# A decoder block on one core: the weight panel's split between the second and third eviction, and the experts' semaphores raised before the attention stage

## What is computed

```python
h = rms_norm(x, g_mix)
z = h @ w_in                      # 1024 x 8208, split into ten column groups
q, k, v, r, a_lr, c_b, c_c, c_x, g_a, g_b = split_columns(z)
o = gla_chunked(q, k, v, log_sigmoid(a_lr @ w_alpha_up + b_alpha) / 16)
y_a = (rms_norm(o, g_gla) * silu(r)) @ w_branch_a
y_b = (c_b * causal_dwconv(c_c * c_x, w_conv)) @ w_branch_b     # 3 taps
x = x + (sigmoid(g_a) * y_a + sigmoid(g_b) * y_b) @ w_out
h = rms_norm(x, g_ffn)
x = x + top-4-of-32 mixture of experts(h)    # clamped SwiGLU, chosen pairs alone
out = rms_norm(x, g_final)
```

## Time and profile before

| | us |
|---|---|
| median of 3 runs | 2753.02 (2749.55 to 2753.60) |
| the profiled execution | 2757.46, its span 2755.8 |
| PE busy | 2550.3 (93%) |
| DVE busy | 1502.2 (55%) |
| ACT busy | 1205.3 (44%) |
| convolution, first panel's last eviction to last panel's | 624.71 to 952.73 |
| join | 955.8 to 1260.3 |
| route, up to its closing barrier | 1260.4 to 1333.7 |
| experts | 1337.3 on |

### The profile page before, as it was taken

One profiled execution on the slowest core, in us unless ns is written; L12 is line 12 of the kernel. 1 busy time (PEld: TensorE's weight loads), 2 busy tenths in 40 slices (PEclk: granted clock), 3 DMA queues, 4 the chain that ended last, 5 costly groups with the idle time before them and its releaser, 6 DMA issues. The chain is left out here.

```text
span 2755.8 us, 41814 instructions
## 1 busy us (share of the span) xinstructions
PE 2550.3 (93%) x14459; PEld 2041.2 (74%) x14460; DVE 1502.2 (55%) x1470; ACT 1205.3 (44%) x1210; POOL 330.5 (12%) x378
## 2 busy tenths in 40 slices
PE   7999999997787898898599999999999999999994
PEld 6987777896676687697367877787867787778773
DVE  5201333332212323424478977788867897678884
ACT  6312343210111101103256766576755676567664
POOL 0000000000000000004411221211221121212110
PEclk9999999999899899996699999999999999999997
DMA  4233233322412221217569998798978999798986
GB/s 112 44 48 47 66 62 67 60 47 32 44 31 37 71 92 61 91 63 262 183 197 332 381 363 302 273 319 305 371 278 293 326 381 345 249 350 316 382 290 214
DMA packets 257660, 536.51 MB, mean 195 GB/s; under 512 B 26624, under 2 KB 74368, under 8 KB 256496
## 3 DMA queue, kind: packets, MB, share of 16 engines
q1 hardware_dynamic: 235552, 485.08, 53.1%
q0 software_dynamic: 20880, 46.15, 6.3%
q10 hardware_dynamic: 1152, 4.19, 0.4%
HBM read 492.72 MB, written 42.63 MB: 194 GB/s over the span
## 5 line engine op out<-in xcount | busy, mean ns | idle before, releaser
L1688 DVE TENSOR_TENSOR m_w_lo<-raw,m_w_hi 128x2048 fp32r<-128x2048 f32 x384 | 874.7, 2289 | 254.7 <-ACT m_w_hi L1592 252.2
L1592 ACT CAST m_w_hi<-raw 128x2048 fp32r<-128x2048 f32 x384 | 731.8, 1907 | 446.6 <-PE m_lin L1827 250.0
L106 PE MATMUL c_bank<-h_hi_r,ring_hi 128*128 128x512 f32 x640 | 264.4, 413 | 66.3 <-DVE ring_raw_r L141 65.3
L108 PE MATMUL c_bank<-h_lo_r,ring_hi 128*128 128x512 f32 x640 | 258.9, 405 | 0.0
L109 PE MATMUL c_bank<-h_hi_r,ring_raw_r 128*128 128x512 f32 x640 | 257.4, 402 | 0.0
L137 ACT CAST ring_hi<-ring_raw 128x2048 fp32r<-128x2048 f32 x44 | 83.8, 1905 | 364.0 <-PE c_bank L109 150.0
L141 DVE TENSOR_TENSOR ring_raw_r<-ring_raw,ring_hi 128x2048 fp32r<-128x2048 f32 x44 | 100.7, 2288 | 249.6 <-ACT ring_hi L137 249.6
L1823 PE MATMUL m_gate<-m_w_hi,m_x_hi 128*128 128x512 f32 x512 | 209.9, 410 | 0.0
L1823 PE MATMUL m_y<-m_w_hi,m_a_hi 128*128 128x512 f32 x512 | 206.0, 402 | 1.5 <-DVE m_a_lo L1740 1.5
L106 PEld LDWEIGHTS c_bank<-h_hi_r,ring_hi 128*128 128x128 f32 x640 | 125.5, 196 | 106.1 <-DVE ring_raw_r L141 70.0
L1827 PE MATMUL m_gate<-m_w_hi,m_x_lo 128*128 128x512 f32 x512 | 201.4, 393 | 0.0
(11 more groups left out here) (306 smaller groups left out, 4621.7 us busy)
## 6 DMA issues: line engine op xcount, KB each, us to landing
raw<-in_w_gate_up SPq DMA_DIRECT2D x512, 512.0 KB, 12.3
raw<-in_w_down SPq DMA_DIRECT2D x256, 512.0 KB, 12.3
ring_raw<-in_w_in SPq DMA_DIRECT2D x32, 1024.0 KB, 9.8
gates<-work POOLq DMA_DIRECT2D x32, 256.0 KB, 3.0
work<-gates SPq DMA_DIRECT2D x8, 1024.0 KB, 6.9
v<-in_x SPq DMA_DIRECT2D x8, 512.0 KB, 10.3
ring_raw<-in_w_branch_b SPq DMA_DIRECT2D x4, 1024.0 KB, 5.2
ring_raw<-in_w_branch_a SPq DMA_DIRECT2D x4, 1024.0 KB, 5.2
```

Source lines behind the costliest of these rows:

```text
L106: pe.matmul(out, left_hi(k), right_hi(k), start=first and k == kts[0], stop=False, skip_group_check=True)
L108: pe.matmul(out, left_hi(k), right_lo(k), start=False, stop=False, skip_group_check=True)
L1592: act.copy(w_hi[:, p % WS].rearrange("p k b n -> p (k b n)"), raw[:, raw_slot(m)].rearrange("p k b n -> p (k b n)")).then_inc(whi, 1)
L1688: dve.tensor_tensor(w_lo[:, p % WS].rearrange("p k b n -> p (k b n)"), raw[:, raw_slot(m)].rearrange("p k b n -> p (k b n)"), f32(w_hi[:, ...
```

## The change

Four edits.

1. Convolution, ACT: in kind 0 `split_hi` of the next panel comes after the second copy, not after the fourth. In kinds 1 and 2 it stays where it was.
2. Convolution, DVE: in kinds 1 and 2 `split_lo` of the next panel comes after the second eviction, so ahead of evictions three and four and of the taps. In kind 0, where DVE evicts nothing, it stays the first thing that DVE does.
3. Join, DVE: `split_lo` of panel n + 1 comes after the second eviction of panel n, for every n but B and A (whose next panels are split elsewhere). In B this is one panel ahead where it was two. ACT's side is untouched.
4. The 43 semaphores are made by a class `Signals`, and POOL raises them right behind `clear_signals`, before the attention stage. The 43 increments and the second barrier between `route` and `experts` are gone; every use is renamed.

```diff
@@ convolution, ACT
                             act.copy(cc[:, r // 2, (r % 2) * HALF:(r % 2 + 1) * HALF],
                                      banks[4 * (n % 2) + r][:, :]).then_inc(cc_done, 1)
+                            if r == 1:
+                                ring.split_hi(act, n + 1)
                     else:
                         act.wait_ge(ready, results(n) + 1)
-                    ring.split_hi(act, n + 1)
+                        ring.split_hi(act, n + 1)
@@ convolution, DVE
                                 .then_inc(u_done, 1)
+                            if r == 1:
+                                ring.split_lo(dve, n + 1)
...
                                               ALU.mult).then_inc(y_done, 1)
-                    ring.split_lo(dve, n + 1)
+                            if r == 1:
+                                ring.split_lo(dve, n + 1)
+                    if kind == 0:
+                        ring.split_lo(dve, n + 1)
@@ join, DVE
                         dve.tensor_tensor(out, part[:, r % 2], out, ALU.add).then_inc(mixed, 1)
-                if n != A - 1 and n != A:
-                    ring.split_lo(dve, n + 2) if n < A - 1 else ring.split_lo(dve, n + 1)
+                    if j == 1 and n != B and n != A:
+                        ring.split_lo(dve, n + 1)
@@ semaphores
+class Signals:
+    def __init__(self, nc, ctx):
...
+        def opened(n):
+            signal = sem(n)
+            nc.gpsimd.sem_inc(signal, OPEN)
+            return signal
+
+        self.raw_loaded = [opened(f"raw_loaded{s}") for s in range(RS)]
+        self.whi = opened("whi")
...
-        for signal in signals:
-            nc.gpsimd.sem_inc(signal, OPEN)
-        nc.all_engine_barrier()
         block = ctx.enter_context(nc.Block())
@@ decoder_block
                 clear_signals(nc)
+                signals = Signals(nc, whole)
```

More of the change, by code:

```diff
@@ L1367, in _, with sem, experts @@
             pe.matmul(turned[0][:, 0:4 * W + 1], ones[:, :], terms[:, :], start=True, stop=True).then_inc(summed, 1)
[L1370 removed]
+class Signals:
+    def __init__(self, nc, ctx):
+        def sem(n):
+            return ctx.enter_context(nc.semaphore(f"m_{n}"))
+        def opened(n):
[4 more added lines that the diff above has]
+        self.whi = opened("whi")
+        self.wlo = opened("wlo")
+        self.picked_gu = opened("picked_gu")
+        self.picked_dn = opened("picked_dn")
+        self.panel_done = opened("panel_done")
+        self.gate_done = opened("gate_done")
+        self.sig = opened("sig")
+        self.gated = opened("gated")
+        self.taken = opened("taken")
+        self.activated = opened("activated")
+        self.turned = opened("turned")
+        self.ahi = opened("ahi")
+        self.alo = opened("alo")
+        self.x_turned = opened("x_turned")
+        self.xhi = opened("xhi")
+        self.xlo = opened("xlo")
+        self.y_stored = opened("y_stored")
+        self.scattered = opened("scattered")
+        self.s_gu = opened("s_gu")
+        self.s_dn = opened("s_dn")
+        self.s_sig = opened("s_sig")
+        self.s_gated = opened("s_gated")
+        self.s_taken = opened("s_taken")
+        self.s_activated = opened("s_activated")
+        self.s_turned = opened("s_turned")
+        self.s_copied = opened("s_copied")
+        self.xs_turned = opened("xs_turned")
+        self.xs_copied = opened("xs_copied")
+        self.s_stored = opened("s_stored")
+        self.waits_met = opened("waits_met")
+        self.rows_in = opened("rows_in")
+        self.in_listed = [sem(f"in_listed{x}") for x in range(2)]
+        self.out_listed = [sem(f"out_listed{x}") for x in range(2)]
+        self.gathered = [sem(f"gathered{x}") for x in range(2)]
+        self.added = [sem(f"added{x}") for x in range(2)]
+def experts(nc, w_gate_up, w_down, h_rows, y_rows, slot_rows, cst, now, where, expert_f, b_split, raw, signals):
     h_quarters = h_rows.rearrange("r (g c) -> (r g) c", g=NG)
@@ L1565, in _ @@
             row, _ = place_of(pool, ahead, 2)
-            list_slots(slot_in, in_listed, row, second)
+            list_slots(slot_in, signals.in_listed, row, second)
             body(0, first=True)
@@ L2097, in decoder_block @@
             raw = late("raw", [P, RS, 2, 2, NW])
-            raw_loaded = [whole.enter_context(nc.semaphore(f"raw_loaded{s}")) for s in range(RS)]
             route(nc, x2, g_ffn, w_router, b_router, b_gate_up, b_down, w_gate_up, w_down, h_rows, y_rows,
-                  slot_rows, cst, now, where, expert_f, b_split, raw, raw_loaded)
-        experts(nc, w_gate_up, w_down, h_rows, y_rows, slot_rows, cst, now, where, expert_f, b_split, raw, raw_loaded)
+                  slot_rows, cst, now, where, expert_f, b_split, raw, signals.raw_loaded)
+        experts(nc, w_gate_up, w_down, h_rows, y_rows, slot_rows, cst, now, where, expert_f, b_split, raw, signals)
         finish(nc, y_rows, g_final, out, cst)
```

299 lines of the change are left out of this document (139 added, 160 removed).

## The result

The changed kernel took 2648.32 us (median of 4 runs, 2646.49 to 2649.91), the kernel before 2752.70 us beside it. The ratio is 0.9623, with a 95% interval of 0.9606 to 0.9639: 104 us faster. The forecast was 2640 us with a range of 2632 to 2660. The profiled execution of after took 2649.01 us (its span 2647.3), 108.5 us less than that of before. The prediction's sum was made against that one, and was 112.8 us.

The account below looks back on a forecast made before the run. PE, busy 93% of the span, was held to lose time only in pauses, mainly for DVE's late panel split, and at lower clock. Terms of 112.8 us off 2757.46 gave 2644.7, so 2640 us for a median; range 2632 to 2660.

Parts of the forecast that it names:

- Convolution, 88.7 us: Convolution: eleven panels take 239.4 us instead of 328.0, saving 65.3 us of waits and 23.4 us mostly of low clock.
- Rival (b): PE's waits go but the clock stays low anyway, so 30.5 us of gain do not come: 2671 us; chance 0.06.
- Slack of the loads: Convolution: even the worst load seen, 15.7 us, has PE's next panel ready 1.9 us before PE asks at 21.76 us.
- Rival (a): Loads eat the slack: four of the convolution's eleven boundaries miss by 3 us, costing 19 us: 2659 us; chance 0.13.
- Its threshold: Convolution: a boundary costs something once a load takes over 17.6 us (21.76 - 4.2).
- rival (d): Slower than before: splits waiting for loads hold up DVE's in-order queue; 30 us loads would give 2777 us; chance 0.02.
- End of the convolution: Barrier after the convolution: comes 2.2 us earlier without the last split, plus 1.7 us from no low clock behind it.
- Join, 16.6 us: Join: three panel boundaries each lose about 5.5 us to waits for the split and low clock; all would be saved.
- the same 5.5 us: Join: the third wait, before the first panel of w_out, was costed at 5.5 us of gain like the first two.
- So no new wait: Join: `m_split`, starting about 1.4 us after PE's panel ends, has its blocks ready before PE reaches them, costing nothing.
- Semaphores, 3.6 us: Between route and experts: without the 43 increments and second barrier, the experts' stage moves up by 3.6 us.
- The sum: Whole kernel: 88.7 + 2.2 + 1.7 + 16.6 + 3.6 = 112.8 us less than the profiled execution's 2757.46 us.

Follow-up runs that it names:

- the edits alone: The kernel before with only the convolution's moved splits, ACT's and DVE's: 2662.32 us, ratio 0.9664, 92.5 us less.
- the extra copies: The changed kernel with one or two more 1 MB panel copies to DRAM ahead of each of the convolution's eleven loads: 2680.84 us with one, 2770.08 with two.

## Why the prediction was right, and where it was not

The time lies in the range, on the side of faster, 8 us above the forecast (0.3%). Point by point:

- **Convolution, 88.7 us: right.** 328.0 - 239.4 = 88.6 us in the trace, 21.76 us per panel, taken from a row of another stage with the same product. That the clock comes back with the pauses was shown by the edits alone (92.5 us for 92.6). Rival (b) falls.
- **Slack of the loads: right.** The worst load of the convolution took 15.0 us and no boundary waited. Rival (a) didn't occur. The prediction left 1.9 us for a load of 15.7 us; 2.5 us were left with 15.0. Its threshold held under the extra copies, where waits appear once a load lands more than 17.6 us behind the panel's end; its price for several late loads in a row, and that of rival (d), was too high by the formula above.
- **End of the convolution: 2.2 us right, 1.7 us right in this pair, partly by luck.** The drain is 2.2 us shorter, PE's pause 1.0 us, and the stretch from the join's barrier to the last eviction of B takes 89.9 us instead of 91.5. But four of the eight traces that keep the old pause of 3.25 us show no fall of the clock behind it, and take 89.9 us as well. The 1.7 us can be gained only from an execution in which the clock falls there.
- **Join, 16.6 us: wrong by 7.5 us.** The first two boundaries gave their 5.5 us each. The third was costed at "the same 5.5 us" and lost 2.0. The step that failed is the one on what takes its place, which looked at `m_split` and ended with "So no new wait". It followed who prepares PE's operands and not who frees PE's banks. DVE's first eviction there needs 4 MB that can't be issued before A ends and take 16.1 us, against the 11.5 us in which PE fills its four banks (1058.3 to 1069.8). The trace of before held the number: the landing was 0.02 us ahead of the eviction. That the time still came near the forecast is in part luck: this loss of 7.5 us was half made up by the 3.5 us of the next point. With that one transfer cut in two the boundary gave 5.0 us.
- **Semaphores, 3.6 us: right.** PE's start is 3.4 to 3.9 us sooner in every trace with edit 4. From route's barrier to the end the five traces with it take 1416.0 us on average and the eight without 1420.5 us, 4.5 us less; the profiled pair happens to differ by 7.1. By that pair 3.5 us came that the sum did not have.
- **The sum.** 112.8 - 7.5 (third boundary) + 3.5 (experts) + 1.4 (ahead of the convolution's first panel) - 1.6 (start of the program) = 108.6 us, the 108.5 of the profiled pair. The last three are differences between executions; the first is a cause. With the 7.5 us put right, the forecast for the median would have been 2647.5; 2648.3 was measured.

## What to carry to other kernels

If an engine is late at a boundary, every transfer that starts at that boundary gets the same delay as cover. Before costing the boundary at its full pause, list the transfers issued there, and compare each landing in the trace with the instruction that needs it: one that lands just ahead of its user is the next wait, even if no view of waits names it. And the work of one engine for another's next panel belongs in the middle of its own evictions, as soon as its data can be there; in the one pair of runs here with late loads in both orders, they cost the attention stage 744.5 us in the new order and 743.8 in the old one.

## What the runs showed of the hardware

- **The same pause lowers the clock in one run and not in another.** The join has three pauses of 2.42, 2.36 and 2.36 us at the start of A, alike in all thirteen traces. Behind them the clock fell to 0.50 twice in four traces (before and after among them), once in six, and not at all in three. The pause of 3.25 us at the join's barrier was followed by a fall in four of the eight traces that have it. With the split ahead of the taps, pauses of 3.0 us stood behind both kinds 1 and 2; panels behind them took 26.7 us where the clock fell and 25.0 where it didn't. Pauses of 3.7 us and more, where the clock was at 1.00, were always followed by 3.4 us or more at 1.2 GHz, the barriers' pauses of 0.93 and 1.05 us never. One pause of 1.92 us (one extra copy) was followed by a fall too.
- **An issue can itself take long.** A load's issue takes SP 0.4 us; with two extra copies (3 MB under way) it took up to 11.8 us, and what stood behind it in SP's queue came late by as much.
- **Halves of a transfer do not land at half of its time.** 4 MB landed after 16.1 us; cut in two, the first 2 MB landed after 11.1 and the second after 15.6. The 1 MB of the panel, issued 0.4 us ahead of them, had landed 5.4 us after its issue, 6.1 us ahead of the first half.
